# Products of qb, kb, vb, gates and xq put between the steps of three attention parts

## The reference

```python
n = rms_norm(h, ln_mix_g[l])
proj = n @ w_in[l]
qa, ka, va, qb, kb, vb, ga, gb = jnp.split(proj, splits, axis=-1)
...
ya = dilated_mixture(qa, ka, va).astype(h.dtype) @ w_branch_a[l]
yb = stick_breaking(qb.reshape(b, s, SB_HEADS, HEAD_DIM),
...
gate_a = jax.nn.sigmoid(ga + b_gate[l, :D_MODEL])
gate_b = jax.nn.sigmoid(gb + b_gate[l, D_MODEL:])
h = h + (gate_a * ya + gate_b * yb) @ w_out[l]
n = rms_norm(h, ln_x_g[l])
m = rms_norm(mem, ln_mem_g[l])
h = h + memory_cross_attn(n, m, w_xq[l], w_xkv[l], w_xo[l])
```

## Time and profile before

| | us |
|---|---|
| three runs, median (lowest, highest) | 4039.75 (4034.96, 4049.16) |
| profiled execution, its own time | 4044.2 |
| its span | 4042.0 |
| PE busy in the span | 3546.6 (88%) |
| DVE, ACT busy | 1965.8, 1195.3 |
| granted PE clock, mean | 0.906 of full speed |

### The profile page before, as it was taken

How to read it: one execution, slowest core, us unless ns; L and a number is a source line. 1 busy time by engine, 2 the same in 40 slices (tenths; PEclk the granted TensorE clock), 3 DMA queues, 4 the chain that set the end, 5 groups by cost and what they waited for, 6 DMA issues and landing times. The chain is left out here.

```text
span 4042.0 us, 50175 instructions
## 1 busy us (share of the span) xinstructions
PE 3546.6 (88%) x22090; PEld 2867.7 (71%) x22090; DVE 1965.8 (49%) x2440; ACT 1195.3 (30%) x1475; POOL 76.2 (2%) x52
## 2 busy tenths in 40 slices
PE   7888579879999999969899988999687777689996
PEld 6657357758887888868788876887466766378885
DVE  5232334547744443455444355443646765754435
ACT  2222432332223222323322233222332322132223
POOL 0000000000000000100100011000000000010001
PEclk9658789969999999989999999999788889799998
DMA  3001002202222222313232222222121000022231
GB/s 148 24 0 63 0 31 101 98 21 99 99 86 91 94 95 93 115 42 105 78 104 88 93 91 73 94 89 69 63 73 39 3 3 3 21 89 94 88 101 51
DMA packets 43416, 284.38 MB, mean 70 GB/s; under 512 B 4800, under 2 KB 4928, under 8 KB 16832
## 3 DMA queue, kind: packets, MB, share of 16 engines
q1 hardware_dynamic: 43200, 281.19, 20.2%
HBM read 279.07 MB, written 2.10 MB: 70 GB/s over the span
## 5 line engine op out<-in xcount | busy, mean ns | idle before, releaser
L427 PE MATMUL ps<-xh,wh 128*128 128x512 f32 x2688 | 1073.0, 399 | 100.5 <-DVE xl L827 43.7
L427 PE MATMUL ps<-xl,wh 128*128 128x512 f32 x2688 | 1062.2, 395 | 0.0
L427 PE MATMUL ps<-xh,wl 128*128 128x512 f32 x2688 | 1061.1, 395 | 0.0
L302 DVE TENSOR_TENSOR wl<-raw,wh 128x2048 fp32r<-128x2048 f32 (+3 forms) x284 | 591.5, 2083 | 474.4 <-ACT wh L297 474.1
L427 PEld LDWEIGHTS ps<-xh,wh 128*128 128x128 f32 x2688 | 512.4, 191 | 239.4 <-issue 119.1
L297 ACT CAST wh<-raw 128x2048 fp32r<-128x2048 f32 (+3 forms) x284 | 492.4, 1734 | 363.0 <-PE ps L427 357.8
L427 PEld LDWEIGHTS ps<-xh,wl 128*128 128x128 f32 x2688 | 512.0, 190 | 111.7 <-issue 2.5
L427 PEld LDWEIGHTS ps<-xl,wh 128*128 128x128 f32 x2688 | 512.9, 191 | 108.5 <-issue 3.0
L427 PE MATMUL ps<-hid_h,wh 128*128 128x512 f32 x880 | 343.0, 390 | 2.8 <-DVE wl L302 2.8
L427 PE MATMUL ps<-hid_l,wh 128*128 128x512 f32 x880 | 342.5, 389 | 0.0
L427 PE MATMUL ps<-hid_h,wl 128*128 128x512 f32 x880 | 342.5, 389 | 0.0
(11 more groups left out here) (332 smaller groups left out, 3986.9 us busy)
## 6 DMA issues: line engine op xcount, KB each, us to landing
raw<-in_up SPq DMA_DIRECT2D x88, 1024.0 KB, 4.8
raw<-in_down SPq DMA_DIRECT2D x64, 704.0 KB, 4.0
raw<-in_up_c SPq DMA_DIRECT2D x22, 1024.0 KB, 4.8
raw<-in_down_c SPq DMA_DIRECT2D x16, 704.0 KB, 4.0
raw<-in_gates SPq DMA_DIRECT2D x8, 1024.0 KB, 4.8
raw<-in_gv SPq DMA_DIRECT2D x8, 1024.0 KB, 4.8
raw<-in_gu SPq DMA_DIRECT2D x8, 1024.0 KB, 4.8
raw<-in_gout SPq DMA_DIRECT2D x8, 1024.0 KB, 4.7
```

The lines of the kernel that those rows point to most:

```text
L302: nc.vector.tensor_tensor(wl[:, slot, 0:w], raw[:, slot, 0:w], wh[:, slot, 0:w].bitcast(F32), ALU.subtract).then_inc(lo_ready, 1)
L427: last = nc.tensor.matmul(out, stationary, moving, start=(fresh and q == 0), stop=(t == kt - 1 and half == per - 1 and q == 2), skip_group ...
```

## The change

`Woven` is a product stage without a block of its own: its parts (`products` of some tiles of one unit, `high` and `low` of the next weight chunk, `evict`) are called from the orders of the attention parts. A unit or lot is 128 output features (for vb 256 features of two token blocks), 24 matmuls of 512 columns (vb: 48 of 256).

In dilated attention the units with b > 0 (12 of 16) take one unit of qb, kb or vb each, in three pieces. Scores have one set of three banks in place of two, transposes two banks in place of one. In stick breaking each head takes two lots of gates; the causal mask goes ahead of the sums, and the next head's passes ahead of the cast of this head's result. The gates are stored before their sigmoid; `open_gates` applies it, four in the last head and twelve in `branch_a`. `branch_b` splits its own result for w_out. The memory's split goes into w_out's second unit, x's split into xv's first. Cross attention runs over four heads with all 512 queries, with one lot of xq for each head between the steps. `between` calls given functions in a unit of `linear`; `here` in `Deferred` makes the split wait for such a call.

```diff
-               tokens=EVERY, last_rows=P, norms=None, sums=False):
+               tokens=EVERY, last_rows=P, norms=None, sums=False, between={}):
...
+                if unit in between and between[unit][0]:
+                    between[unit][0](act)
...
+    class Woven:
+
+        def __init__(self, name, kt, xs, banks, evict, steps=0, token_blocks=0):
+            self.a, self.count, self.kt, self.xs, self.banks = first[name], count_of[name], kt, xs, banks
+            self.part, self.token_blocks = evict, token_blocks
+            self.units = 2 * self.count
+            chunks[0] = self.a + self.count
+            psum_read.stage(1, self.units)
+            lot_done.stage(1, self.count)
+            self.read, self.lot = psum_read.base, lot_done.base
+
+            @block.sync
+            def _(sp):
+                for n in range(self.a, self.a + self.count):
+                    sp.wait_ge(lo_ready, n + 1)
+                    load(sp, n + 2)
+
+        def bank(self, unit):
+            return self.banks[(self.read + unit) % len(self.banks)]
+
+        def high(self, act, chunk):
+            n = self.a + chunk + 1
+            split_hi(act, n, 16 * (n // 2 + 1), n % 2, order[n][2])
+
+        def low(self, dve, chunk):
+            n = self.a + chunk + 1
+            split_lo(dve, n, n % 2, order[n][2])
+
+        def products(self, pe, unit, t0, t1):
+
+            chunk, lot = unit // 2, unit % 2
+            slot, b = (self.a + chunk) % 2, self.bank(unit)
+            if t0 == 0:
+                pe.wait_ge(psum_read.sem, self.read + unit + 1 - len(self.banks))
+                pe.wait_ge(lo_ready, self.a + chunk + 1)
+            for t in range(t0, t1):
+                hi, lo = self.xs(t)
+                if self.token_blocks:
+                    wc = slice(t * 256, (t + 1) * 256)
+                    for m in range(2):
+                        xc = slice((2 * lot + m) * P, (2 * lot + m + 1) * P)
+                        out = ps[:, b, m * 256:(m + 1) * 256]
+                        fresh = t == 0 and m == 0
+                        nc.tensor.matmul(out, hi[:, xc], wh[:, slot, wc], start=fresh, stop=False, skip_group_check=True)
+                        nc.tensor.matmul(out, hi[:, xc], wl[:, slot, wc], start=False, stop=False, skip_group_check=True)
+                        last = nc.tensor.matmul(out, lo[:, xc], wh[:, slot, wc], start=False, stop=(t == self.kt - 1),
+                                                skip_group_check=True)
+                else:
+                    wc = slice(t * 256 + lot * P, t * 256 + (lot + 1) * P)
+                    nc.tensor.matmul(ps[:, b, :], wh[:, slot, wc], hi, start=(t == 0), stop=False, skip_group_check=True)
+                    nc.tensor.matmul(ps[:, b, :], wh[:, slot, wc], lo, start=False, stop=False, skip_group_check=True)
+                    last = nc.tensor.matmul(ps[:, b, :], wl[:, slot, wc], hi, start=False, stop=(t == self.kt - 1),
+                                            skip_group_check=True)
+            if t1 == self.kt:
+                last.then_inc(chunks_used if lot else lot_done.sem, 1)
+
+        def evict(self, engine, unit):
+
+            chunk, lot = unit // 2, unit % 2
+            if lot:
+                engine.wait_ge(chunks_used, self.a + chunk + 3)
+            else:
+                engine.wait_ge(lot_done.sem, self.lot + chunk + 1)
+            self.part(engine, unit, ps[:, self.bank(unit), :]).then_inc(psum_read.sem, 1)
...
+    qb_rows = Woven("qb", KD, x_split, (0, 4), feature_rows(qb, HD ** -0.5))
+    kb_rows = Woven("kb", KD, x_split, (0, 4), feature_rows(kb, 1.0))
+    vb_tokens = Woven("vb", KD, x_split, (0, 4), vb_rows, token_blocks=TB)
+    rows_read = psum_read.total
...
+    beside = {}
+    for u in range(len(units)):
+        if units[u][1]:
+            n = len(beside)
+            beside[u] = ((qb_rows, kb_rows, vb_tokens)[n // 4], n % 4)
...
-            if u >= 2:
-                pe.wait_ge(da_masked.sem, da_masked.after(u - 2, 3))
+            if u >= 1:
+                pe.wait_ge(da_masked.sem, da_masked.after(u - 1, 3))
...
+        def turn(u, lot):
+            n_lot = 3 * u + lot
+            if n_lot >= 2:
+                pe.wait_ge(da_moved.sem, da_moved.base + n_lot - 1)
+            blocks = key_blocks(units[u][1])
+            c0 = P * sum(len(x) for x in blocks[:lot])
+            for n, _ in enumerate(blocks[lot]):
+                last = nc.tensor.transpose(ps[:, 5 + n_lot % 2, n * P:(n + 1) * P], probs[:, c0 + n * P:c0 + (n + 1) * P],
+                                           table("ident"))
+            last.then_inc(da_turned.sem, 1)
...
+            fill(u, 0, 3)
+            pe.wait_ge(da_norm.sem, da_norm.after(u, 1))
+            turn(u, 0)
+            turn(u, 1)
+            fill(u, 3, 6)
+            turn(u, 2)
+            fill(u, 6, 8)
             weigh(u)
...
+            if u in beside:
+                rows_of, unit = beside[u]
+                if rows_of is not vb_tokens:
+                    rows_of.evict(dve, unit)
             low(u)
+            if u in beside and unit % 2 == 0:
+                rows_of.low(dve, unit // 2)
...
+            if u in beside:
+                rows_of, unit = beside[u]
+                if rows_of is vb_tokens:
+                    rows_of.evict(act, unit)
             rows, cols = slice(HD * (j % 2), HD * (j % 2) + HD), slice(b * P, (b + 1) * P)
             act.wait_ge(da_out.sem, da_out.after(u, 1))
             nc.scalar.copy(ya_h[rows, j // 2, cols], ps[rows, 7, 0:P]).then_inc(da_high.sem, 1)
...
-    linear("qb", KD, 256, x_split, dve_part=scaled_tiles(qb, first_norm, rs, HD ** -0.5))
-    linear("kb", KD, 256, x_split, dve_part=scaled_tiles(kb, first_norm, rs))
-    linear("vb", KD, 256, x_split, act_part=to_tokens(vb, first_norm, TB), token_blocks=range(TB))
...
+    gate_lots = Woven("gates", KD, x_split, (3,), gate_rows)
...
         for hd in range(SBH):
             if hd + 1 < SBH:
                 logits(hd + 1)
+            gate_lots.products(pe, 2 * hd, 0, KD)
             after(hd)
+            gate_lots.products(pe, 2 * hd + 1, 0, KD)
             weigh(hd)
...
+        copy_logits(0)
+        logs(0)
+        for hd in range(SBH):
+            gate_lots.high(act, hd)
             if hd + 1 < SBH:
                 copy_logits(hd + 1)
-            act.wait_ge(sb_arg.sem, sb_arg.after(hd, 7))
+            act.wait_ge(sb_arg.sem, sb_arg.after(hd, 3))
             nc.scalar.activation(stick[:, :], stick[:, :], ACT.Exp).then_inc(sb_a.sem, 1)
+            if hd + 1 < SBH:
+                logs(hd + 1)
+            else:
+                open_gates(act, 0, 4)
             act.wait_ge(sb_out.sem, sb_out.after(hd, 1))
-            nc.scalar.copy(yb_h[lane(hd), hd // 2, :], ps[lane(hd), 6 + hd % 2, :]).then_inc(sb_high.sem, 1)
+            nc.scalar.copy(yb_h[lane(hd), hd // 2, :], ps[lane(hd), 7, :]).then_inc(sb_high.sem, 1)
 
...
+            for c in range(TB):
+                nc.vector.tensor_tensor(stick[:, SB[c]:SB[c] + P], stick[:, SB[c]:SB[c] + P], table("causal"),
+                                        ALU.add).then_inc(sb_open.sem, 1)
+            if hd:
+                low(hd - 1)
+            gate_lots.evict(dve, 2 * hd)
+            dve.wait_ge(sb_open.sem, sb_open.after(hd, 4))
             dve.wait_ge(sb_after.sem, sb_after.after(hd, 1))
             for b, o, n in LINES:
-                nc.vector.tensor_tensor(stick[:, o:o + n], stick[:, o:o + n], ps[:, 3 + b, 0:n],
+                nc.vector.tensor_tensor(stick[:, o:o + n], stick[:, o:o + n], ps[:, 4 + b, 0:n],
                                         ALU.subtract).then_inc(sb_arg.sem, 1)
-            dve.wait_ge(sb_arg.sem, sb_arg.after(hd, 3))
-            for c in range(TB):
-                nc.vector.tensor_tensor(stick[:, SB[c]:SB[c] + P], stick[:, SB[c]:SB[c] + P], table("causal"),
-                                        ALU.add).then_inc(sb_arg.sem, 1)
...
+            gate_lots.low(dve, hd)
+            gate_lots.evict(dve, 2 * hd + 1)
+        low(SBH - 1)
...
+    def mix_high(act, k, products, u):
+        act.wait_ge(dve_steps.sem, dve_steps.after(k, 1))
+        for m in range(2):
+            last = nc.scalar.copy(xh[:, 2 * k + m, :], mix[:, 2 * k + m, :])
+        last.then_inc(act_steps.sem, 1)
...
-    linear("gates", KD, 256, x_split, act_part=gate_act, dve_part=gate_dve, steps=(1, 1))
-    linear("branch_a", 2, D, lambda t: (ya_h[:, t, :], ya_l[:, t, :]), dve_part=gated_a)
-    linear("branch_b", 4, 512, lambda t: (yb_h[:, t, :], yb_l[:, t, :]), dve_part=gated_b, steps=(0, 1))
-    linear("w_out", KD, 256, x_split, norms=Halves(mix, KD, x_split), **summing(onto_h(2), h, 2))
+    linear("branch_a", 2, D, lambda t: (ya_h[:, t, :], ya_l[:, t, :]), dve_part=gated_a,
+           between={0: (lambda act: open_gates(act, 4, 2 * KD), None)})
...
```

(57 more changed lines are left out.)

355 lines of the change are left out of this document (198 added, 157 removed).

## The result

The changed kernel takes 3850.2 us (median of 4 runs, 3848.4 to 3852.3) against 4042.1 us (4035.0 to 4049.2, 4 runs) for the kernel before on the same chip. The ratio is 0.952, with a 95% interval of 0.951 to 0.953. The forecast of 3838 us is 12 us (0.3%) too low, and its range holds the result.

A forecast was written before the change was run, and what follows sets the result against it. Products on TensorE, busy 88% of 4042.0 us, were taken to bound most of the kernel. Savings of 44 + 119 + 3 + 4 + 32 = 202 us from 4044.2 gave 3842, less 4.5 for the median: 3838 us, range 3810 to 3870.

The forecast's parts named there:

- Dilated part: Dilated attention with qb, kb, vb products: 252.0 us before, 196 + 9 + 3 = 208 after, 44 saved; bounds 161 and 310.
- Stick breaking with gates: Stick breaking with gates lots inside each head: 284.3 us before, TensorE becomes the bound at 19.9 us a head, 119 saved.
- the 165 us forecast: Stick breaking with gates after the change: 159 us for eight heads, plus 1.5 start, 1.5 end, 3 slow stretches.
- Branches, w_out and keys: Branches, w_out and memory keys, 115.4 us before: smaller gaps save 3 ahead of w_out and 4 of 7.7 us later.
- xq and cross attention: xq lots between cross attention's steps: 83.3 us before, 51 after, 32 saved; bounds 45 and 65.
- A: Rival: fills keep the clock up throughout; 173 us in the dilated part, 3 less elsewhere, 3800 us; 15%.
- B: Rival: the dilated part keeps its clock of 0.59, scores and transposes standing between short fills; 3916 us; 15%.
- Its half with 0.55 slow: Milder case of rival B: 0.55 of the dilated part's work runs slow, 3877 us.
- That rule: Rule against the forecast: transposes do not count as activity releasing the clock, so they cut the fills; rival B would result.
- C: Rival: DVE or ACT sets the period in stick breaking; at 23.6 us a head 3862 us; 12%.
- its short form: Within rival C: longer stalls in the first part, with which the total is 3880 us.
- D: Rival: slow clock stays in dilated part and stick breaking, mean about 0.6, 627 us against 536.3; 4121 us; 3%.

The follow-up runs named there:

- The run with the units apart: Changed kernel with all twelve units of qb, kb and vb products behind the dilated part instead of inside it: 3876.0 us, ratio 0.9575.
- even lots: Changed kernel with weight splits early and qb, kb, vb products in equal lots of six tiles beside all sixteen dilated units: 3817.4 us, ratio 0.9433.
- the program that differs only further on: Even lots and early splits, with `low` of xq's third lot moved behind the normalisation of head 1 in cross attention: 3822.5 us, ratio 0.9445.

## Why the prediction was right

**Dilated part, 208 us forecast, 206.9 measured.** The sum is right through two errors that nearly cancel, and of the idle time it gave too much to the fills.
- `weigh` at full clock was taken as 0.71 of its slow time (0.156 us each) from a group of cross attention that had the clock only partly up. It takes 2.40 us for 20, 0.12 each: 54 x 4 x 0.036 = 7.8 us less work at full clock, 153 us in place of 161.
- The slow clock then costs 193.6 - 153 = 41 us, where a quarter of the work at half speed was put at 35. Its place was forecast well: the b = 0 blocks, the scores behind them, the start of the fill after. The clock itself was put lower, near 0.75, and is 0.82.
- The waits: 9 us at four units before the normalisation, measured 9.5 at those four; 3 us for the rest, measured 13.3 - 9.5 = 3.8. The single bank for scores was put at nothing and costs one wait of 0.8 us.
- The shorter wait for the copies was given to the two banks and to the fills together. The run with the units apart parts them: the banks and the order bring 14.2 of the 15.2 us before the transposes without any fill, and the fills bring 6.8 of the 8.2 before `weigh`. The weight splits ate that gain, so on balance the fills brought the clock alone.
- Why the clock falls at b = 0 stays open. No single condition tried here is both enough and needed: it falls there with the waits gone (0.50 from 188 to 200 us with the splits moved), is up for the scores behind it when a fill stands beside (3.71 us for 2,048 columns), and stayed up once at b = 3 with no fill.

**Stick breaking with gates, 119 us forecast, 111.9 measured.** This term was mis-sized by 7 us, the largest miss of the four stages. The window of 95.45 us of before that the sum set against the forecast holds 24 products of branch_a, 5.45 us, and the 165 us forecast had none: 170.5 was the like figure. The rest is the head: 20.18 us and not 19.9, 8 x 0.28 = 2.2 us. Start, end and low clock took 172.4 - 161.4 - 5.45 = 5.5 us, forecast 6. (The wait for `mix` before branch_a's 25th product lies in this stage too, 0.55 us where it was 2.70.) The mechanism, TensorE as the bound with no idle time before `after`, is what the trace shows. The two halves of it that the prediction did not part are 44.5 us (order) and 67.3 (lots between).

**Branches, w_out and keys, 7 us forecast, 11.4 measured.** The gap ahead of w_out fell from 4.37 us to 1.12, as forecast (3). Ahead of xk it fell from 4.96 to 1.18, and ahead of xq from 2.72 to 2.28. The wait for the sums of `mem_norm` that the prediction moved there shows as 2.35 us. By the run with the split put back 2.1 to 3.3 us belong to it; the forecast had 4 for that edit. The idle time of the stage went from 13.1 to 6.9 us (window less busy), so 6.2 us saved, near the forecast of 7. What the sum left out is busy time: 102.3 to 97.1 us, 5.2 us, with the clock at 1.00 where it was 0.93. In the kernel before the clock was low behind the gaps: 0.70 in the 5.7 us from branch_a's 25th product, 0.57 in the 6.2 us from w_out's first and 0.50 in the 5 us from xk's first; in the first profile of the changed kernel the smaller gaps did not lower it. That is not so in every execution: in the second profile the stage is 105.3 us, with 100.2 busy at a clock of 0.97.

**xq and cross attention, 32 us forecast, 34.6 measured.** The waits were named and priced well: 1.77 us before the transposes of head 1 (forecast 2), 3.24 + 0.67 after head 3 (forecast 5.5). Which part brings the gain was not said in numbers: 24.6 us are the larger step and its order, 10.0 the lots between.

**The rest, 0 forecast, -9.4 measured,** with -1.5 ahead of the part and +1.4 in xo. No effect of the change is shown there: the second profile of the same kernel has 6.7 us of the rest back, and -0.4 in xo.

Together: 202 forecast, 201.5 in the four stages; the 9.5 us less in the span are the last item. That the four agree to 0.5 us is luck: they missed by 0.4, 7.1, 4.4 and 2.6 us, the first two below the forecast and the last two above it. The medians differ by 191.9 us, 10 less than forecast, and the kernel before read 2.3 us more beside the changed one than in the runs shown; these make the 12 us.

**The rivals.** A (clock kept up throughout, 173 us in the dilated part) did not come in this kernel, but even lots reach 177.3. B (the dilated part keeps 0.59) fell: with fills the clock is 0.82, and the variant without them has 0.58. (Its half with 0.55 slow comes to 3873 us with B's own 5 us of waits, not 3877.) Fills with transposes and scores between them held the clock at 1.00 from 156 to 184 us. The Trainium skill, "TensorE: Matmul & The Clock Gate", Part 4: PE-mode transpose, says that a PE-mode transpose does not count as busy time in the same way. That rule did not decide here. Whether a transpose counts for nothing or for little, no run here separates from the scores. C (DVE or ACT sets the period) fell with 20.18 us a head and no idle time; in the dilated part its short form is the 9.5 us. D fell with clocks of 0.82 and 0.98.

## What to carry to other kernels

Where attention leaves TensorE at half clock, full-height products that exist anyway are worth more between its steps than behind them, and here most in thin, even lots: the same products gave 28.5 us beside twelve units, 8.6 more with the splits early, and 21.0 more beside all sixteen units (13 to 15 in the program that differs only further on). Put the other engines' share of those products (splits, evictions) behind the attention step that TensorE will ask for next; the splits at the wrong place cost 8.6 us, in four waits. Before pricing an overlap, price the order alone: here 15 us of 43.6, 44.5 of 111.9 and 24.6 of 34.6 needed no product of another stage between the steps.

## What the runs showed of the hardware

The granted clock of one program differs between executions with nothing else changed. The untouched 3.15 ms took 3155.2 and 3148.5 us in two profiles of the same kernel, with TensorE busy for 2829.9 and 2819.7 us at a clock of 0.93 and 0.94. The Trainium skill, "TensorE: Matmul & The Clock Gate", Part 1, calls the number of matmuls that run slow after a start run-variable for the same kernel. These rows do not count such matmuls; they show a variation of the same kind in a whole stretch, 6.7 us in 3.15 ms. A reader of one profile should not explain less than that, nor a microsecond or two in one of the stages here.

A clock once low can stay low while TensorE is busy throughout: in the run with the splits early it was 0.50 for 12.00 us of 12.00 busy in the b = 0 stretch, where the scores of 32 rows take 7.19 us. It had fallen with no wait over 0.4 us in the 11 us before, so a long wait is not needed for the fall. And a missing fill is not enough to lose the clock: with fills beside b = 0, 1 and 2, `weigh` of b = 3 ran in 2.40 us in one slot and in 4.46 in another, the latter behind a wait of 3.94 us.
